# VectorE transposes inside a triangular inverse, the last doubling of both directions side by side, and a later residual load

## The reference, cut to what matters

```python
a_mat = where(strict, einsum(kb, k) * gamma, 0)          # per head and chunk
t_mat = a_mat + eye(C)
u = triangular_solve(t_mat, v * beta)                    # so the inverse of t_mat is applied
w = triangular_solve(t_mat, kb * exp(gc))
v_new = u_n - w_n @ S;  o = q_dec @ S + qk @ v_new;  S = S * g_last + k_dec^T @ v_new
o_na = neighborhood_attention(q_na, k_na, v_na, rpb)     # second mixer, 16 rows of 64 tokens
mix = concatenate([o_gdn, o_na]) @ w_out
x = layer_norm(ALPHA * x + mix, ln1_g, ln1_b)            # then the MLP, blocks two and three
```

## Time and profile before

| | us |
|---|---|
| median of 3 runs | 4027.97 (4024.52 to 4028.22) |
| the profiled execution | 4026.77 |
| its span | 4025.0 |
| TensorE busy | 3889.9 (97%) |
| VectorE busy | 2177.2 (54%) |
| ScalarE busy | 1673.6 (42%) |
| mean granted TensorE clock | 0.992 |

### The profile page before, as it was taken

The page is one execution under the profiler, slowest core; times in us unless marked ns, Lnnn a source line. Parts: engine busy times, 40 slices in busy tenths (PEclk is TensorE's granted clock), DMA queues, the critical chain, the costliest instruction groups (busy, mean ns, idle before and its releaser), DMA issues.

```text
span 4025.0 us, 49987 instructions
## 1 busy us (share of the span) xinstructions
PE 3889.9 (97%) x20780; PEld 3147.9 (78%) x20780; DVE 2177.2 (54%) x3288; ACT 1673.6 (42%) x2626; POOL 17.1 (0%) x34
## 2 busy tenths in 40 slices
PE   4999999998999999999999999999999999999999
PEld 2777788886788877878778878977777777778887
DVE  6541565555633456874747746346646346646333
ACT  3351566764433354443534334233335233334333
POOL 0000000000000000000000000000000000000000
PEclk9999999998999999999999999999999999999999
DMA  4112000022242222222222222222222222223222
GB/s 168 48 58 75 11 7 8 21 71 86 79 120 95 94 89 84 74 89 94 85 89 74 90 89 89 86 90 78 83 84 94 89 89 79 79 89 112 96 95 86
DMA packets 113880, 323.61 MB, mean 80 GB/s; under 512 B 26920, under 2 KB 34040, under 8 KB 113656
## 3 DMA queue, kind: packets, MB, share of 16 engines
q1 hardware_dynamic: 111416, 314.91, 23.7%
q0 software_dynamic: 2240, 5.51, 0.7%
HBM read 303.86 MB, written 18.06 MB: 80 GB/s over the span
## 4 chain that ended last, share of the span: by engine, by line
PE 91%; DVE 4%; ACT 3%; issue 1%; DMA 1%; SPq 0%; DVEq 0%; ACTq 0%
PE ps L311 49%; PE ps L289 25%; PE ps L1036 2%; PE ps L1327 2%; PE ps L1030 1%; PE ps L1304 1%; PE ps L1042 1%; PE ps L725 1%; PE ps L2423 1%; ACT n_s L1359 1%; PE ps L1863 1%; PE ps L1312 1%; PE ps L421 1%; DVE a L508 0%; PE ps L1352 0%
## 5 line engine op out<-in xcount | busy, mean ns | idle before, releaser
L311 PE MATMUL ps<-a,w_hi 128*128 128x512 f32 (+1 forms) x6128 | 1876.4, 391 | 15.1 <-DVE a L508 6.7
L311 PEld LDWEIGHTS ps<-a,w_hi 128*128 128x128 f32 x6128 | 1126.9, 189 | 289.4 <-issue 28.1
L311 PE MATMUL ps<-a,w_lo 128*128 128x512 f32 (+1 forms) x3064 | 1164.1, 386 | 0.0
L262 DVE TENSOR_TENSOR w_lo<-w_raw,w_hi 128x1024 fp32r<-128x1024 f32 x539 | 658.2, 1221 | 448.8 <-ACT w_hi L257 446.0
L257 ACT ACTIVATE w_hi<-w_raw 128x1024 fp32r<-128x1024 f32 x539 | 563.6, 1050 | 555.8 <-DMA w_raw<-in_w_mlp 339.3
L311 PEld LDWEIGHTS ps<-a,w_lo 128*128 128x128 f32 x3064 | 571.2, 189 | 122.7
L289 PE MATMUL ps<-h_hi,w_hi 128*128 128x512 f32 x1536 | 490.0, 401 | 1.9 <-DVE xT L361 1.9
L289 PE MATMUL ps<-h_hi,w_lo 128*128 128x512 f32 x1536 | 481.8, 395 | 0.0
L289 PE MATMUL ps<-h_lo,w_hi 128*128 128x512 f32 x1536 | 481.4, 395 | 0.0
L356 DVE TENSOR_TENSOR h_lo<-u_sq,h_hi 128x512 fp32r<-128x512 f32 x192 | 133.0, 692 | 490.9 <-ACT h_hi L346 490.9
L361 DVE TENSOR_TENSOR xT<-xT,ps 128x1024 f32<-128x1024 f32 x192 | 234.2, 1220 | 289.0 <-PE ps L289 288.2
(11 more groups left out here) (358 smaller groups left out, 3324.1 us busy)
## 6 DMA issues: line engine op xcount, KB each, us to landing
w_raw<-in_w_mlp SPq DMA_DIRECT2D x384, 512.0 KB, 3.3
w_raw<-in_w_in SPq DMA_DIRECT2D x107, 512.0 KB, 3.3
w_raw<-in_w_out SPq DMA_DIRECT2D x48, 512.0 KB, 3.3
xT<-in_x SPq DMA_DIRECT2D x2, 2048.0 KB, 12.9
x<-xT SPq DMA_DIRECT2D x2, 2048.0 KB, 7.6
xT<-x SPq DMA_DIRECT2D x2, 2048.0 KB, 12.5
rpb_rows<-in_rpb SPq DMA_DIRECT2D x1, 3810.0 KB
z<-staged SPq DMA_DIRECT2D x4, 512.0 KB, 3.7
```

Of the source, the lines that this page charges most:

```text
L262: nc.vector.tensor_tensor(w_lo[u.z][:, :], w_raw[u.z][:, :], w_hi[u.z][:, :].bitcast(F32), ALU.subtract).then_inc(w_split[u.z], 1)
L311: last = nc.tensor.matmul(ps[:, bank, 0:t1 - t0], w[:, k * P:(k + 1) * P], a[:, h, low, k, t0:t1], start=(i_k == 0 and i == 0), stop=(i_k ...
```

## The change

1. At l = 1 to 5 VectorE writes `g_D` by one transpose instruction of 128x512 for each direction (it transposes 32x32 blocks, and at these levels all that is read of the blocks lies within them). `turned` of `g_Dt` on TensorE and the copy on ScalarE are gone. At l = 6 VectorE transposes only one 32-row block by four heads of 32 columns for each direction.
2. At l = 6 both products work on the 64x64 corner that counts: `last_level` issues 8 matmuls for both directions together, each direction in its own corner of the array, and waits for both directions first. ScalarE copies the first product to `g_gu` (no mask), VectorE subtracts 64 partitions by 256.
3. The waits that freed PSUM bank 0 for the transposes move to its next users: `S` to slot 6, `R` to slot 10, `kd` to slot 12.
4. Behind the loop: what `end1_act` and `end1_dve` did for pieces 6 and 7 and for token half 1 becomes a segment `late1` of four steps, beside the output units 1 to 4 of half 0. The split of unit 3 now comes between them instead of behind all of them.
5. SP loads only half 0 of the residual ahead of the output weights; half 1 comes behind the first four weight tiles (`residual_sp`).

```diff
+            def last_level(i, lhsT, rhs, rows, done):
+                for h in range(GH):
+                    for d in range(2):
+                        part = side(rows(d))
+                        last = nc.tensor.matmul(pbank(gbank(d, i))[side(d), h, side(1 - d)], lhsT[d][part, h, side(d)],
+                                                rhs[d][part, h, side(1 - d)], start=True, stop=True)
...
-                        turned(turn_bank(d, l), g_Dt[d]).then_inc(gs["tr"], 1)
-                    for d in range(2):
...
-                        half_heads(gbank(d, 1), g_A[d], g_Dt[d], l, 1 - d).then_inc(gs["Q"], 1)
+                        if l < NL - 1:
+                            half_heads(gbank(d, 1), g_A[d], g_Dt[d], l, 1 - d).then_inc(gs["Q"], 1)
+                    if l == NL - 1:
+                        last_level(1, g_A, g_Dt, lambda d: 1 - d, gs["Q"])
...
-                        act.wait_ge(gs["tr"], upper(n, d, l))
-                        nc.scalar.activation(four(g_D[d][:, :, :]), ps[:, turn_bank(d, l), :], ACT.Copy).then_inc(gs["D"], 1)
+                        nc.scalar.activation(g_gu[d][side(d), :, side(1 - d)], pbank(gbank(d, 1))[side(d), :, side(1 - d)], ACT.Copy)\
+                            .then_inc(gs["lev"], 1)
...
+                        dve.wait_ge(gs["Dt"], level(n, d, l - 1))
+                        if l < NL - 1:
+                            nc.vector.transpose(four(g_D[d][:, :, :]), four(g_Dt[d][:, :, :])).then_inc(gs["D"], 1)
+                        else:
+                            upper_rows, lower_rows = quads(d)
+                            nc.vector.transpose(g_D[d][lower_rows, :, upper_rows], g_Dt[d][upper_rows, :, lower_rows]).then_inc(gs["D"], 1)
...
-            for h in range(2):
-                sp.dma_start(tokens(h), g["x1"][:, :, h * HALF:(h + 1) * HALF]).then_inc(x_landed[h], 16)
+            residual_sp(sp, 0)
...
-        rest = [(u, ()) for u in out1[0]]
+        rest = beside([(u, ()) for u in out1[0]], 1, "late1", LATE_STEPS)
```

More of the change, by code:

```diff
@@ L967, in last_once, with side @@
             return once(n, 1 - d if n == TC - 1 else d)
[L969 to L973, removed]
+        def side(d):
+            return slice(GRID * d, GRID * d + GRID)
         def level(n, d, l):
@@ L1003, in halves, with quads @@
             return t.rearrange("p h (n a b) -> p h n a b", a=2, b=1 << l)[:, :, :, which, :]
+        def quads(d):
+            first = GRID * d + 32 * d
+            return slice(first, first + 32), slice(first + 32 - 64 * d, first + 64 - 64 * d)
         def quarters(l):
-            if l == NL - 1:
-                return [(slice(0, P), slice(0, 1))]
             n = GRID >> l + 1
@@ L1034, in half_heads @@
                 for h in range(GH):
-                    for side, pairs in quarters(l):
-                        last = nc.tensor.matmul(halves(pbank(b), l, which)[side, h, pairs], lhsT[side, h, side],
-                                                halves(rhs[:, :, :], l, which)[side, h, pairs], start=True, stop=True)
-                return last
+                    for part, pairs in quarters(l):
+                        last = nc.tensor.matmul(halves(pbank(b), l, which)[part, h, pairs], lhsT[part, h, part],
+                                                halves(rhs[:, :, :], l, which)[part, h, pairs], start=True, stop=True)
+                return last
+            def last_level(i, lhsT, rhs, rows, done):
[4 more added lines that the diff above has]
+                                                rhs[d][part, h, side(1 - d)], start=True, stop=True)
+                        if h == GH - 1:
+                            last.then_inc(done, 1)
             def turned(b, src):
@@ L1107, in gdn_pe @@
                     for d in range(2):
+                        pe.wait_ge(gs["R"], once(n, d))
                         turned(gbank(d, 0), g_kT[:, :, toks(chunk_of(n, d))]).then_inc(gs["kt"], 1)
@@ L1111, in gdn_pe @@
                         pe.wait_ge(gs["gu"], once(n + 1, d))
+                        if n >= 0:
+                            pe.wait_ge(gs["kd"], once(n, d))
                         nc.tensor.matmul(ps[:, gbank(d, 0), :], const("ones"), four(g_vn[d][:, :, :]), start=True, stop=True)\
@@ L1213, in gdn_dve @@
                     for d in range(2):
[L1214 to L1218, removed]
+                        dve.wait_ge(gs["Dt"], level(n, d, l - 1))
+                        if l < NL - 1:
+                            nc.vector.transpose(four(g_D[d][:, :, :]), four(g_Dt[d][:, :, :])).then_inc(gs["D"], 1)
+                        else:
+                            upper_rows, lower_rows = quads(d)
+                            nc.vector.transpose(g_D[d][lower_rows, :, upper_rows], g_Dt[d][upper_rows, :, lower_rows]).then_inc(gs["D"], 1)
+                    for d in range(2):
+                        if l < NL - 1:
+                            dve.wait_ge(gs["Q"], upper(n, d, l))
+                            nc.vector.tensor_tensor(halves(g_gu[d][:, :, :], l, 1 - d), halves(pbank(gbank(d, 1)), l, 1 - d), lev_mask(l, d), ALU.mult)\
+                                .then_inc(gs["lev"], 1)
                 if 1 <= s <= 12 and s % 2 == 0 and n >= 0:
+                    if l == NL - 1:
+                        dve.wait_ge(gs["X"], upper(n, 1, l))
                     for d in range(2):
                         dve.wait_ge(gs["X"], upper(n, d, l))
[L1222 to L1225, removed]
+                        for part, pairs in quarters(l) if l < NL - 1 else [(side(d), slice(0, 1))]:
+                            block = halves(g_Dt[d][:, :, :], l, 1 - d)[part, :, pairs]
+                            ins = nc.vector.tensor_tensor(block, block, halves(pbank(gbank(d, 2)), l, 1 - d)[part, :, pairs], ALU.subtract)
                         ins.then_inc(gs["Dt"], 1)
@@ L1559, in end1_act @@
             mix1_hi(act, 0, (4, 5, 6, 7))
[L1560 to L1566, removed]
         def end1_dve(dve):
@@ L1572, in end1_dve, with late1_act, late1_dve @@
             mix1_lo(dve, 0, (4, 5, 6, 7))
+        LATE_STEPS = 4
+        def late1_act(act):
+            out_rs(act, 6, SUM_BANKS[6])
+            out_rs(act, 7, SUM_BANKS[7])
+            yield
+            act.wait_ge(gs["o"], 2 * TC)
+            act.wait_ge(na["of"], ROWS)
+            mix1_hi(act, 1, (0, 1, 2, 3))
+            yield
+            act.wait_ge(go["end"], 8)
+            mix1_hi(act, 1, (4, 5, 6, 7))
+            yield
+            yield
+        def late1_dve(dve):
+            yield
             out_norm(dve, 6)
             out_norm(dve, 7)
-            mix1_lo(dve, 1, range(DC))
+            yield
+            mix1_lo(dve, 1, (0, 1, 2, 3))
+            yield
+            mix1_lo(dve, 1, (4, 5, 6, 7))
+            yield
         def bias_sp(sp):
@@ L2795, in build_program @@
         segment("na", na_pe, na_act, na_dve)
+        segment("late1", None, late1_act, late1_dve)
         segment("gout", gout_pe, gout_act, gout_dve)
@@ L2951, in _ @@
                 load_sp(sp, u)
+            residual_sp(sp, 1)
             for u in order[FIRST1 + SLOTS:]:
```

21 lines of the change are left out of this document (11 added, 10 removed).

## The result

The changed kernel takes 4019.41 us (median of 20 runs, 4014.34 to 4023.22), the kernel before 4026.99 (20 runs on the same chips): ratio 0.998, 95% interval 0.9973 to 0.9987. That is 7.6 us where 45 were forecast, and outside the range. The profiled execution took 4014.57 us, its span 12.2 us less than before's; it is the second fastest of the 20, so the profiles show some 4.6 us more gain than the medians.

The account below looks back on a forecast made before the run. TensorE, busy 97% of the span, bounds the kernel until VectorE's chain ends last. Loop 41.8 + tail 13.8 - clock 8 - transpose pairs 2 = 45.6 us off 4026.77: 3981, metric 3982; 8 in 10: 3965 to 4008.

Parts of the forecast that it names:

- the clock term: In the loop TensorE's clock falls after about half the steps, some 2 us each: 8 us of gain lost.
- the transpose: VectorE's 128x512 transpose takes 0.69 us, a pair 1.28; 0.1 more per pair, three pairs a step, costs 2 us.
- both weak places: Between first and second product TensorE is busy 2.0 of 4.75 us at level 4, 2.0 of 3 at level 1.
- Rival A: In the loop the clock falls more than once every step, costing 3 to 4 us each: 3998 to 4006; chance 0.15.
- My own condition for being wrong: Wrong if a transpose exceeds 1 us, steps stay above 56 us, or the loop's clock falls below 0.9.
- rival B: VectorE transposes at half rate, 1.22 us: 4 us a step, 33 in all, so 4012; chance 0.13.
- Level 6 side by side: Level 6's two products, in alternating corners, take 0.53 us each instead of 1.73, 2.4 us less TensorE work a step.
- The re-timed step: One plain chunk step, interval by interval, takes 53.6 us after the change, a gain of 4.3.
- The six intervals of the prediction: Parts of one plain step, first mask to next first mask: 8.4 + 7.7 + 15.0 + 3.1 + 8.5 + 11.0 us.
- the late steps: Steps with output norms: n = 5 gains 5.5 us, n = 6 8.0, n = 7 up to kt 6.8.
- The seam: Behind kt of the last step: 6.3 to the fold, 5.6 and 1.9 at the fourth output unit, 13.8 us gained.

Follow-up runs that it names:

- idle278: Changed kernel plus 4 unread whole 128x128 TensorE transposes ahead of the second product in slots 2 and 8 and at slot 7's end: 3985.67 us, ratio 0.9898.
- idle28: Changed kernel plus 4 unread whole 128x128 TensorE transposes ahead of the second product in slots 2 and 8 only: 3992.53 us, ratio 0.9915.
- pe_turns: Changed kernel with the transposes of levels 1 to 5 back on TensorE and their copies on ScalarE: 3998.66 us, ratio 0.9926.
- tail_only: Kernel before with only the parts behind the loop changed (`late1`, half 1 of the residual behind four weight tiles): 4017.25 us, ratio 0.9974.
- fill278: Changed kernel with the first product's corner matmuls reissued, unread, before the second product in slots 2, 8 and at slot 7's end: 3991.33 us, ratio 0.9908.

## Why the prediction was wrong

**The step that failed is the clock term**: "the lower level after about half the steps, some 2 us each: 8 back". The balance from first mask of n = 0 to kt of n = 7: before 887.67 - 427.94 = 459.7, after 885.03 - 426.28 = 458.8. A gain of 1.0 where 41.8, less 8 for the clock and 2 for the transpose, was forecast. By steps: the five plain ones lost 6.6, n = 5 lost 2.1, n = 6 gained 6.7, n = 7 up to kt 3.0. So 40.8 us are missing. What the clock took of it can be added up from steps in which it held: 52.2 for n = 0 (idle278), 53.85 for each of n = 1 to 4, 56.4 for n = 5 (idle28), 58.75 for n = 6 (the changed kernel itself), and 38.3 for n = 7 up to kt (idle28, one fall left in it) make 421.0, where the changed kernel takes 458.8. So the clock term, which I had at 8, is near 38 us; the other 3 us are steps that are a little longer at full clock than forecast. Both factors of the term were too small. I had named both weak places (between the products of levels 1 and 4) but counted one fall in two steps: in n = 1 to 5 both places fall in every step. And I priced a fall at 2 us, from one row of the kernel before. Its loop has a second fall, in n = 7, that I didn't look at, and it is longer:
```profile
853.35 1.94 PE L1312 MATMUL ps<-consts,n_s 128*128 128x128 f32 x8 [1.23 <-ACT n_pt L1367]
858.77 3.78 PE L1327 MATMUL ps<-n_v,n_pt 128*128 128x128 f32 x16
```
These two and the two groups between them take 4.3 us more than the same groups at full clock (0.9, 0.9, 0.8 and 1.7). In the changed kernel n = 1 to 4 lose 4.7 to 7.6 us each against 53.85. In n = 3 (58.5, so 4.7 lost) the groups at half pace make up 4.3 of it: 0.9, 0.8 and 1.1 us in 609 to 616, 1.5 in the key-query product.

Rival A had the mechanism and, at 0.15, too little chance; even it, at 3 to 4 us a step, stopped short (3998 to 4006). The argument that I held against it, a quick return to full clock, was true and beside the point: what counts is that it happens each time. The Trainium skill (TensorE: Matmul & The Clock Gate, "HAM oscillation"), which the prediction passed on to rival A, names the pattern, for a loop that waits for DMA. The trace agrees: the clock falls and returns within each step but one, and is 0.86 to 0.91 on average in the stretches above. Here pauses of 1.2 and 1.3 us between products were enough. My own condition for being wrong ("if steps stay above 56 us") is what came.

**What was right.** The transpose: 0.684 us for 0.69, so rival B is out, and with it the estimate of 1.24 us from the 311 ns of the Trainium skill (VectorE: DVE Perf Modes, "The three transpose paths"). Level 6 side by side: 0.68 us a group with its end, 0.61 to the next instruction (0.53 forecast), and 2.7 us a step by pe_turns against tail_only, of the 3.3 forecast. The re-timed step: 53.85 measured in idle28 where the clock holds, 53.6 forecast, so the chain over VectorE was at most 0.25 longer than worked out. (The six intervals of the prediction add up to 53.7 as printed; and n = 6's Q of level 2, which it has at 13.95 before, stands 13.88 behind the mask.) In n = 3 the intervals that no fall touches came out nearly as worked: Q of level 5 to kt 3.1 for 3.1, kt to `g_dec` 8.9 for 8.5, on to the mask 11.1 for 11.0; those with a fall in them did not: 9.5 for 8.4, 9.7 for 7.7, 16.2 for 15.0. In n = 2 of idle28, at full clock, the same three are 8.3, 7.8 and 14.6. Of the late steps n = 6 gave 6.7 of 8.0; n = 5 and 7, with falls, not.

**The seam.** The kernel after, behind kt:
```profile
885.03 1.97 PE L1054 MATMUL ps<-consts,mixT 128*128 128x128 f32 x8
888.41 0.61 SPq L1689 DMA_DIRECT2D xT<-x  x1
899.43 1.06 ACT L257 ACTIVATE w_hi<-w_raw 128x1024 fp32r<-128x1024 f32 x1 [0.93 <-DMA w_raw<-in_w_out]
906.13 1.97 PE L1376 MATMUL ps<-consts,n_z 128*128 128x64 f32 x8 [6.71 <-DVE n_z L1477]
958.78 2.29 DVE L489 TENSOR_TENSOR mixh<-xT 128x2048 f32<-128x2048 f32 x1
```
The split comes 11.0 us behind the residual's issue (17.1 before), the fold 21.1 behind kt (26.2, so 5.1 gained where 6.3 were forecast), the fourth unit without a pause. In the kernel before the same L489 stands at 974.46, 86.8 behind its kt; now it is 73.75 behind. 13.0 gained, 13.8 forecast; in tail_only, with the old loop, it is 75.2, so 11.6 gained.

**A loss behind it that I had not looked for.** At L489 the changed kernel is 15.7 us ahead, at the end 12.2. The same waits of TensorE in both, before first, then after:
```profile
1806.29 1.98 PE L2010 MATMUL ps<-c_sq,consts 128*128 128x512 f32 x4 [2.30 <-DVE c_sq L2068]
1928.14 1.13 PE L421 MATMUL ps<-mixh,consts 128*128 128x512 f32 x2 [2.31 <-DVE mixh L447]
```
```profile
1791.97 3.02 PE L2052 MATMUL ps<-c_sq,consts 128*128 128x512 f32 x4 [2.29 <-DVE c_sq L2110]
1915.47 1.92 PE L421 MATMUL ps<-mixh,consts 128*128 128x512 f32 x2 [2.31 <-DVE mixh L447]
```
The lead is 14.3 us at the first, 12.7 at the second. The code there is the same and so are the pauses (2.30 and 2.29); one run's clock fell behind it and the other's did not. At the next such wait it is the other way round: the kernel before takes 2.07 us there (pause 2.50) and the changed one 1.12 (pause 2.78). The profiles of all twelve experiments look like the changed kernel's: the first row takes 2.47 to 3.05 us in them, the second 1.31 to 1.96. So the same pause costs 1 to 2 us or nothing. Why is not shown: that it hangs on when the pause comes is a guess, and what sets the kernel before apart from all the others is the seam.

## What to carry to other kernels

Work that is taken off a full TensorE is won only if what takes its place doesn't leave it pausing: here short pauses of 1.2 and 1.3 us, two in a step of some 59 us, ate the gain of the transposes removed from it. Move work off it at the places where enough other work stands between producer and consumer, and keep it where too little does; and before a redesign try the cheap probe, idle matmuls in the pause: the steps in which the clock then holds show what the loop is worth. In the profile compare the mean duration of one unchanged matmul group and the clock column, since a half-clocked engine looks as busy as ever.

## What the runs showed of the hardware

VectorE transposes 128x512 of fp32, in blocks of 32x32, in 684 ns, as long as the usual plain pass over 512 elements here (0.69; the cheapest took 0.48). Matmuls in alternating 64x64 corners with 64 columns take 0.68 us for 16 records, where the 16 records of the whole form took 1.90. Adding 12 whole idle transposes to each step of the changed kernel makes it 33.7 us faster (3985.67 against 4019.41): work that nothing reads paid for itself many times over in a kernel whose TensorE is busy 96% of the span. And a stretch may be busy 5.00 of 5 us and still be followed by a lower clock, as in fill278 around its slot 8:
```profile
500.00:505.00 5.00, 5.00 (x87) 4.20 (x85) 4.80 (x18) 1.09 (x2) 0.00 (x0) 1.00 0.12 26
505.00:510.00 5.00, 4.74 (x75) 4.50 (x75) 3.10 (x9) 3.29 (x9) 0.00 (x0) 0.69 0.02 5
```
